# Column halves for the small products of a chunked delta-rule solve, and a first modulation sum split between TensorE and VectorE

## Chip, cores and metric

The kernel runs on one core of a Trainium2 chip. The metric is the device time of one execution in microseconds (us), a median over runs. Engines: TensorE (PE in the rows, PEld for its weight loads), VectorE (DVE), ScalarE (ACT), GpSimd (POOL), and SyncE (SP), which here only issues DMA transfers.

## What is computed

A decoder block on 512 tokens of width 1024, all in f32. Cut to the two places that matter here:

```
mod = c @ w_ada + b_ada
shift, scale, gate = split(mod, 3)
h = rmsnorm(x, pre_norm_gain) * (1.0 + scale) + shift
proj = h @ w_in                       # queries, keys, values, gates of two branches
...
# gated delta rule, 8 heads, key and value width 128, chunks of 64 tokens
lower = where(strict, (kb @ k.T) * decay, 0)
t_mat = triangular_solve(lower + eye, eye, unit_diagonal=True)
...
out = x + gate * rmsnorm(y @ w_o, post_norm_gain)
```

The queries are normalised by the root of their sum of squares per token; that sum is `ssq` below. The other branch is a sparse attention with 8 heads.

## The kernel before

**Layout.** Tokens are in four tiles of 128 (index i, NT = 4), the width in eight blocks of 128 (index k, KT = 8). PSUM is one tensor `ps` of eight banks of 512 columns. The large projections run in "units" of 128 output columns, each split into a high and a low part, so that a unit is 24 products of 512 columns (lines 723 to 725). TensorE goes through rounds; a round is a quarter of a unit (six products), and behind it come small products of the delta-rule heads, the attention and so on, at round numbers written out by hand (`solve(h, r - R_DELTA[h])`). Each engine has its own program with the same rounds; `Steps` gives every instruction of one kind a number on a semaphore, and a waiting instruction holds up all that is behind it on its engine.

**The prologue** (first 50 us). SyncE loads x, then for each block k the eight row blocks of `w_ada` for shift and scale (`mod_rows[:, k % 5, j, :]`, j = 0 to 7, in two halves of 512 KB with a semaphore each, line 511), then the first weights (line 516). The modulation of block k is a sum over 1024 rows: ScalarE scales row block 0 by its entry of c (`first_row`, line 1087) into PSUM, VectorE adds row blocks 1 to 7 (`mod_sum`, line 1607), TensorE sums over the 128 partitions by a product with ones (`modulation`, line 778), and VectorE adds the biases (`mod_columns`, lines 1613 and 1615). ScalarE then makes h of block k from x, transposed by TensorE (`turn`, line 769; h at line 1107, its high part at 1110), and the first products start (line 703). VectorE scales x's four token tiles by their norms (line 1593) before and between the sums of block 0. ScalarE's queue holds, in this order: the squares of x, `first_row(0)`, four copies of rotary tables (lines 1095, 1098), `first_split(0)`, `first_row(1)`, `first_split(1)` (line 1073), and h of block 0. VectorE's queue: sums of block 0, the first two sums of block 1, `mod_columns(0)`, the other sums of block 1.

**The solve of a head** (`solve`, one head each 33 us or so from 160 to 415 us). The inverse U of a unit triangular 128x128 block per token tile is put together from blocks of 16, 32 and 64. U and its transpose T come from DRAM with 32x32 diagonal parts done. The steps on TensorE, each over the four tiles:

- Z32 and dU32 (lines 866, 875): 32-column products on two tiles of the array on its diagonal, (rows 0 to 63, columns 0 to 31) and (rows 64 to 127, columns 64 to 95), and the like.
- `ssq` (line 889): q2 of a tile as stationary operand, a column of ones moving; result column i in bank 5. ScalarE copies it out (line 1236).
- Z64 (line 894): L times the upper right part of U, stationary 128 rows by 64 columns, result in partitions 0 to 63 of bank 3. VectorE copies it to Zs (line 1863).
- T32 (line 898): U transposed whole, 128x128, into bank 4. ScalarE copies all of it to T (line 1239).
- dU64 (line 910): T (64x64) times Zs, result in partitions 0 to 63 of bank 3; VectorE adds it to U (line 1867), which the scan of the head reads three rounds later (line 923).

vT (line 904) transposes the values in between. Which part of the array a product uses follows from where its operands and its result lie: the partitions of the operands give the rows of the array, those of the result in PSUM give the columns.

Of the kernel before, what the change touches and what calls it, by code (L numbers as in the profile page):

```python
# [15 lines left out]
P = 128  # L16
# [147 lines left out]
def program(nc, ctx, x, positions, first_cols, w_mod, w_gate, b_gate, post_gain, w_first, w_units, cst_in, cols_in, out):  # L164
# [144 lines left out]

    def o_row(t):  # L310

        return ps[:, 2 * t:2 * t + 2, :].rearrange("p a b -> p (a b)")
# [18 lines left out]
    def gvec(slot, h):  # L331
        return gsc[:, slot, :, h]

# [26 lines left out]
    def steps(name, names):  # L360
# [23 lines left out]
    pro_pe = steps("pro_pe", ["tables", "x0", "x1", "mod0"]  # L384
# [4 lines left out]
                    + ["xn0", "xn1", "xn2"] + [f"row{j}_0" for j in range(1, 4)] + ["xn3"] + [f"row{j}_0" for j in range(4, KT)]  # L389
# [305 lines left out]
    def _(pe):  # L695
# [66 lines left out]
        def turn(k):  # L762

            if k == 0:
                pe.wait_ge(*pro_dve.at(f"xn{NT - 1}"))
            if k >= 2:
                pe.wait_ge(*pro_act.at(f"h{k - 2}"))
            for i in range(NT):
                mm = pe.transpose(ps[:, 6 + k % 2, blk(i)], x_sb[:, i, blk(k)], ident)
            mm.then_inc(*pro_pe.inc(f"x{k}"))  # L770

        def modulation(k):

            if k == 0:
                pe.wait_ge(*pro_pool.at("ones"))
            pe.wait_ge(*pro_dve.at(f"row{KT - 1}_{k}"))
            for n in range(2):
                mm = pe.matmul(ps[:, 4 + k % 2, 2 * P + n:2 * P + n + 1], mod_rows[:, k % GROUPS, 0, n * P:(n + 1) * P], ones_p[:, 0:1],
                               start=True, stop=True)
            mm.then_inc(*pro_pe.inc(f"mod{k}"))  # L780

        turn(0)
        turn(1)
        modulation(0)
# [61 lines left out]
        def solve(h, rel):  # L846
# [36 lines left out]
            elif rel == 10:  # L883
# [175 lines left out]
    def _(act):  # L1059
# [23 lines left out]
        def first_row(k):  # L1083
            act.wait_ge(s_mod[k % GROUPS][0], (k // GROUPS + 1) * 16)
            if k >= 2:
                act.wait_ge(*pro_dve.at(f"scale{k - 2}"))
            act.activation(ps[:, 4 + k % 2, 0:2 * P], mod_rows[:, k % GROUPS, 0, :], ACT.Copy,
                           scale=pcol[:, 0, R_C:R_C + 1]).then_inc(*pro_act.inc(f"row{k}"))
# [136 lines left out]
        def solve(h, rel):  # L1225
# [316 lines left out]
    def _(dve):  # L1542
# [53 lines left out]
        def mod_sum(k, js):  # L1596

            acc = ps[:, 4 + k % 2, 0:2 * P]
            for j in js:
                if j == KT // 2:  # L1600
                    dve.wait_ge(s_mod[k % GROUPS][1], (k // GROUPS + 1) * 16)
                if j == 1:
# [3 lines left out]
                total = mod_rows[:, k % GROUPS, 0, :] if j == KT - 1 else acc  # L1606
# [3 lines left out]
        def mod_columns(k):  # L1610

            dve.wait_ge(*pro_pe.at(f"mod{k}"))
            dve.tensor_tensor(small_cols[:, 8 + k:9 + k], ps[:, 4 + k % 2, 2 * P:2 * P + 1], pcol[:, 0, R_BADA + k:R_BADA + k + 1],
# [228 lines left out]
        def solve(h, rel):  # L1842
# [278 lines left out]
```

## Time and profile before

| | us |
|---|---|
| median of 3 runs | 814.15 |
| lowest and highest run | 814.05, 814.99 |
| the profiled execution's own time | 814.45 |
| its span, first to last instruction | 812.5 |
| TensorE busy | 778.4 (96%) |
| VectorE busy | 444.2 (55%) |
| ScalarE busy | 338.5 (42%) |
| GpSimd busy | 400.4 (49%) |

The span leaves out what lies before the first and after the last instruction, 1.95 us here. A row of the timeline merges neighbouring instructions of one line: it gives the start of the first, the time from there to the end of the last, and their count. Since products overlap in the array, the end of one lies behind the start of the next; what a product takes from TensorE is the distance from its start to the start of the next.

### The profile page before, as it was taken

To read this page: it belongs to the slowest core of one execution; us is meant where nothing else is said; L and a number is where in the kernel's file an instruction comes from. 1 tells how busy PE (TensorE), PEld (TensorE's weight loads), DVE (VectorE), ACT (ScalarE), POOL (GpSimd) and SP (SyncE) were. 2 spreads that over 40 slices of the span, in tenths; PEclk is the share of its full clock that TensorE was granted. 3 is DMA by queue.
4 is the path that set the end of the run, shared out by engine and by line. 5 is a ranking of instruction groups with operands and counts; after the bars stand their busy time and mean duration, and the time that the engine had idled before them with its cause. 6 is when DMAs were issued, how large, how long until landed. Compare 5 with 4: busy or idle time off the path is not lost.

```text
span 812.5 us, 11490 instructions
## 1 busy us (share of the span) xinstructions
PE 778.4 (96%) x4176; PEld 631.2 (78%) x4176; DVE 444.2 (55%) x992; ACT 338.5 (42%) x719; POOL 400.4 (49%) x348
## 2 busy tenths in 40 slices
PE   2998998999999899999999999999999999999997
PEld 2877874777877688878888777778777788878997
DVE  6858779767588966877754243343334233331114
ACT  5576544534544345345344444343442432222131
POOL 3665542375545445566435254355355355434451
PEclk8899999999999999999999999999999999999999
DMA  8945545333344142312211212221222245432602
GB/s 330 413 146 190 166 96 207 102 117 103 99 87 112 66 111 92 104 66 92 78 60 71 79 53 78 78 79 55 75 85 73 95 157 187 156 129 79 230 4 103
DMA packets 69495, 95.53 MB, mean 118 GB/s; under 512 B 32936, under 2 KB 45608, under 8 KB 69440
## 3 DMA queue, kind: packets, MB, share of 16 engines
q1 hardware_dynamic: 69440, 94.81, 35.5%
q8 instruction: 33, 0.54, 0.3%
q14 instruction: 22, 0.18, 0.1%
HBM read 85.02 MB, written 9.22 MB: 116 GB/s over the span
## 4 chain that ended last, share of the span: by engine, by line
PE 78%; DVE 12%; ACT 5%; issue 2%; DMA 1%; POOL 1%; SPq 0%; DVEq 0%; POOLq 0%; ACTq 0%
PE ps L723 18%; PE ps L725 18%; PE ps L724 18%; PE ps L997 2%; PE ps L1051 2%; PE ps L1050 2%; PE ps L1049 2%; PE ps L984 2%; ACT prob L1318 2%; DVE binv L1836 2%; DVE prob L1947 1%; DVE yq L1760 1%; PE ps L991 1%; PE ps L709 1%; PE ps L703 1%
## 5 line engine op out<-in xcount | busy, mean ns | idle before, releaser
L1416 POOL TENSOR_TENSOR w_lo<-raw,w_hi 128x512 fp32r<-128x512 f32 x210 | 283.6, 1374 | 296.4 <-ACT w_hi L1069 296.4
L723 PE MATMUL ps<-h_hi,w_hi 128*128 128x512 f32 x648 | 274.3, 423 | 0.0
L725 PE MATMUL ps<-h_hi,w_lo 128*128 128x512 f32 x648 | 254.9, 393 | 0.0
L724 PE MATMUL ps<-h_lo,w_hi 128*128 128x512 f32 x648 | 254.0, 392 | 0.0
L723 PEld LDWEIGHTS ps<-h_hi,w_hi 128*128 128x128 f32 x648 | 122.5, 189 | 29.8 <-issue 9.4
L725 PEld LDWEIGHTS ps<-h_hi,w_lo 128*128 128x128 f32 x648 | 122.1, 188 | 27.5
L724 PEld LDWEIGHTS ps<-h_lo,w_hi 128*128 128x128 f32 x648 | 122.7, 189 | 21.9 <-issue 2.2
L1069 ACT ACTIVATE w_hi<-raw 128x1024 fp32r<-128x1024 f32 x105 | 109.7, 1054 | 17.1 <-PE ps L1051 17.1
L1254 ACT ACTIVATE o_tok<-ps 128x128 f32<-128x128 f32 x32 | 8.9, 278 | 89.7 <-PE ps L949 89.6
L1050 PE MATMUL ps<-w_lo,y_hi 128*128 128x256 f32 x128 | 36.2, 283 | 0.0
L1051 PE MATMUL ps<-w_hi,y_lo 128*128 128x256 f32 x128 | 36.2, 283 | 0.0
L1049 PE MATMUL ps<-w_hi,y_hi 128*128 128x256 f32 x128 | 36.2, 283 | 0.0
L1952 DVE SCALAR_TENSOR_TENSOR oat<-ps,za 128x512 f32<-128x512 f32 x8 | 5.5, 691 | 56.0 <-PE ps L997 56.0
L1346 ACT ACTIVATE y_hi<-ysum 128x512 fp32r<-128x512 f32 x8 | 5.1, 632 | 72.1 <-DVE ysum L1975 72.1
L1964 DVE SCALAR_TENSOR_TENSOR ysum<-th_b,ps 128x512 f32<-128x512 f32 x8 | 5.5, 686 | 50.4 <-PE ps L725 50.4
L1318 ACT ACTIVATE prob<-prob,amx 128x128 f32<-128x128 f32 (+3 forms) x32 | 17.6, 552 | 29.7 <-DVE amx L1940 29.7
L1753 DVE MAX8 m<-score 128x8 f32<-128x256 f32 (+2 forms) x48 | 26.4, 550 | 0.0
L1755 DVE MATCH_REPLACE8 score<-m,score 128x256 f32<-128x256 f32 (+2 forms) x48 | 26.1, 543 | 0.0
L723 PE MATMUL ps<-ob_hi,w_hi 128*128 128x512 f32 x64 | 25.1, 392 | 0.0
L723 PE MATMUL ps<-oa_hi,w_hi 128*128 128x512 f32 x64 | 25.0, 391 | 0.0
L724 PE MATMUL ps<-oa_lo,w_hi 128*128 128x512 f32 x64 | 24.9, 389 | 0.0
L724 PE MATMUL ps<-ob_lo,w_hi 128*128 128x512 f32 x64 | 24.9, 389 | 0.0
(275 smaller groups left out, 1378.5 us busy)
## 6 DMA issues: line engine op xcount, KB each, us to landing
raw<-in_w_units SPq DMA_DIRECT2D x105, 512.0 KB, 3.2
mod_rows<-in_w_mod SPq DMA_DIRECT2D x16, 512.0 KB, 8.7
inverse_tiles<-zero SPq DMA_DIRECT2D x12, 344.0 KB, 5.1
ada<-in_w_gate SPq DMA_DIRECT2D x8, 512.0 KB, 4.6
x_sb<-in_x SPq DMA_DIRECT2D x4, 512.0 KB, 6.0
first_raw<-in_w_first SPq DMA_DIRECT2D x8, 256.0 KB, 7.3
L<-gc_rows SPq DMA_DIRECT2D x8, 256.0 KB, 4.4
lower_tiles<-L SPq DMA_DIRECT2D x8, 256.0 KB, 2.7
```

Source lines behind the costliest of these rows:

```text
L723: pe.matmul(out_ap, w_hi[:, slot, k, :], rhs_hi(k), start=(k == 0), stop=False)
L724: pe.matmul(out_ap, w_hi[:, slot, k, :], rhs_lo(k), start=False, stop=False)
L725: mm = pe.matmul(out_ap, w_lo[:, slot, k, :], rhs_hi(k), start=False, stop=(k == KT - 1))
L984: pe.matmul(ps[:, SB[qt], 0:n], qk[:, 0, blk(qt)], qk[:, 1, 0:n], start=True, stop=True).then_inc(*attend_pe.inc(f"s{qt}"))
L1049: pe.matmul(o_ap, y_hi[k][:, blk(t)], w_hi[:, pair, k, :], start=(k == 0), stop=False)
L1050: pe.matmul(o_ap, y_hi[k][:, blk(t)], w_lo[:, pair, k, :], start=False, stop=False)
L1051: mm = pe.matmul(o_ap, y_lo[k][:, blk(t)], w_hi[:, pair, k, :], start=False, stop=(k == KT - 1))
L1069: act.activation(w_hi[:, slot], raw[:, slot], ACT.Copy).then_inc(hi_made, 1)
L1318: act.activation(prob[:, keys(qt)], prob[:, keys(qt)], ACT.Exp, bias=amx[:, 1, qt:qt + 1], scale=HD ** -0.5, accum_out=amx[:, 2, qt:qt + 1 ...
L1416: ins = pool.tensor_tensor(w_lo[:, slot, ks], raw[:, slot, ks], w_hi[:, slot, ks].bitcast(F32), ALU.subtract)
L1753: dve.max(m8[:, t, :], w).then_inc(*top_dve.inc(f"max{t}"))
L1755: dve.match_replace(w, m8[:, t, :], w, TAKEN).then_inc(*top_dve.inc(f"take{t}"))
```

## The change

Two edits. In the solve, `ssq` is done as two products per tile, one per half of the stationary columns, each with its result on one half of the partitions. Z64, T32 and dU64 put the results of even tiles on partitions 0 to 63 and of odd tiles on partitions 64 to 127, two tiles side by side in the columns; T32 transposes only the 64x64 corner that dU64 reads, as a product with a 64x64 identity. The copies become one of 128x128 elements (Zs, T), and the addition to U becomes two, for even and odd tiles. In the prologue, row blocks 0 to 3 of block k = 0 are summed by eight products on TensorE that take c's column as moving operand (`first_modulation`, in bank 7, ahead of the transposes); ScalarE scales row block 4 instead of 0, VectorE adds 5 to 7, and two small additions bring the direct sums into the biases (`direct_columns`). The transposes of x block 1 go behind the modulation of block 0.

```diff
-    pro_pe = steps("pro_pe", ["tables", "x0", "x1", "mod0"]
+    pro_pe = steps("pro_pe", ["tables", "direct", "x0", "mod0", "x1"]
...
-                    + ["xn0", "xn1", "xn2"] + [f"row{j}_0" for j in range(1, 4)] + ["xn3"] + [f"row{j}_0" for j in range(4, KT)]
+                    + ["xn0", "xn1", "xn2"] + [f"row{j}_0" for j in (5,)] + ["xn3"] + [f"row{j}_0" for j in (6, 7)] + ["direct0", "direct1"]
...
+    MOD_DIRECT = KT // 2
+    def first_mod(k):
+        return MOD_DIRECT if k == 0 else 0
...
+            elif k == 1:
+                pe.wait_ge(*pro_dve.at("direct1"))
...
+        def first_modulation():
+            pe.wait_ge(s_mod[0][0], 16)
+            pe.wait_ge(s_rows, 16)
+            for n in range(2):
+                for j in range(MOD_DIRECT):
+                    mm = pe.matmul(ps[:, 7, n:n + 1], mod_rows[:, 0, j, n * P:(n + 1) * P], pcol[:, 0, R_C + j:R_C + j + 1],
+                                   start=(j == 0), stop=(j == MOD_DIRECT - 1))
+            mm.then_inc(*pro_pe.inc("direct"))
+        first_modulation()
         turn(0)
+        modulation(0)
         turn(1)
-        modulation(0)
...
-                    mm = pe.matmul(ps[:, 5, i:i + 1], q2[:, blk(i)], ones[:, 0:1], start=True, stop=True)
+                    for half in (slice(0, 64), slice(64, P)):
+                        mm = pe.matmul(ps[half, 5, i:i + 1], q2_tiles[:, i, half], ones[:, 0:1], start=True, stop=True)
...
-                    mm = pe.matmul(ps[0:64, 3, upper(i)], L[:, h, i, 0:64], U[:, par, i, 64:P], start=True, stop=True)
+                    half, at = slice(64 * (i % 2), 64 * (i % 2) + 64), slice(64 * (i // 2), 64 * (i // 2) + 64)
+                    mm = pe.matmul(ps[half, 3, at], L[:, h, i, 0:64], U[:, par, i, 64:P], start=True, stop=True)
...
-                    mm = pe.transpose(ps[:, 4, blk(i)], U[:, par, i, :], ident)
+                    mm = pe.matmul(ps[half, 4, at], U[0:64, par, i, 0:64], ident[0:64, 0:64], start=True, stop=True)
...
-                    mm = pe.matmul(ps[0:64, 3, upper(i)], T[0:64, i, 0:64], Zs[0:64, i, 64:P], start=True, stop=True)
+                    mm = pe.matmul(ps[half, 3, at], T[half, i // 2, 0:64], Zs[half, i // 2, 0:64], start=True, stop=True)
...
-            act.wait_ge(s_mod[k % GROUPS][0], (k // GROUPS + 1) * 16)
+            act.wait_ge(s_mod[k % GROUPS][first_mod(k) // (KT // 2)], (k // GROUPS + 1) * 16)
...
-                act.activation(T[:], tiles(bank(4)), ACT.Copy).then_inc(*solve_act.inc("T32"))
+                act.activation(T[:, 0:2, 0:64], halves(ps[:, 4, 0:P]), ACT.Copy).then_inc(*solve_act.inc("T32"))
...
+        def direct_columns():
+            dve.wait_ge(*pro_pe.at("direct"))
+            for n, bias in ((0, pcol[:, 0, R_BADA:R_BADA + 1]), (1, small_cols[:, 16:17])):
+                at = small_cols[:, 8 + 8 * n:9 + 8 * n]
+                dve.tensor_tensor(at, ps[:, 7, n:n + 1], bias, ALU.add).then_inc(*pro_dve.inc(f"direct{n}"))
...
-        mod_sum(0, range(1, 4))
+        mod_sum(0, (5,))
         scale_rows(3)
-        mod_sum(0, range(4, KT))
+        mod_sum(0, (6, 7))
+        direct_columns()
...
-                dve.tensor_copy(Zs[0:64, :, 64:P], tiles(bank(3))[0:64, :, 64:P]).then_inc(*solve_dve.inc("Z64"))
+                dve.tensor_copy(Zs[:, 0:2, 0:64], halves(ps[:, 3, 0:P])).then_inc(*solve_dve.inc("Z64"))
...
-                dve.tensor_tensor(U[0:64, par, :, 64:P], U[0:64, par, :, 64:P], tiles(bank(3))[0:64, :, 64:P],
-                                  ALU.add).then_inc(*solve_dve.inc("U64"))
+                for odd in range(2):
+                    of_turn = U[0:64, par, odd::2, 64:P]
+                    ins = dve.tensor_tensor(of_turn, of_turn, halves(ps[64 * odd:64 * odd + 64, 3, 0:P]), ALU.add)
+                ins.then_inc(*solve_dve.inc("U64"))
```

## Rows read from the trace of the kernel before

**Rows 1.** The page: busy us, share of the span, instructions.

```profile
PE 778.4 (96%) x4176; PEld 631.2 (78%) x4176; DVE 444.2 (55%) x992; ACT 338.5 (42%) x719; POOL 400.4 (49%) x348
```

**Rows 2.** Waits of TensorE, 160-420 us: total, times, longest.

```profile
PE ps L942 <- DVE vnew L1875: 3.3, 4, 2.1
```

**Rows 3.** Timeline of TensorE, head 0: start, us, instructions; last row: cut at 173.2.

```profile
172.29 0.39 PE L724 MATMUL ps<-h_lo,w_hi 128*128 128x512 f32 x1
172.52 0.40 PE L725 MATMUL ps<-h_hi,w_lo 128*128 128x512 f32 x1
172.84 0.68 PE L894 MATMUL ps<-U,L 128*64 128x64 f32 x8
173.45 0.66 PE L898 MATMUL ps<-cst,U 128*128 128x128 f32 x4
173.86 0.48 PE L723 MATMUL ps<-h_hi,w_hi 128*128 128x512 f32 x1
...
177.26 0.68 PE L910 MATMUL ps<-Zs,T 64*64 64x64 f32 x8
177.87 0.50 PE L723 MATMUL ps<-h_hi,w_hi 128*128 128x512 f32 x1
...
172.84 0.56 PE L894 MATMUL ps<-U,L 128*64 128x64 f32 x6
```

**Rows 4.** Timeline of TensorE, head 1, around ssq.

```profile
205.40 0.95 PE L889 MATMUL ps<-cst,q 128*128 128x1 f32 x8
206.21 0.48 PE L723 MATMUL ps<-h_hi,w_hi 128*128 128x512 f32 x1
```

**Rows 5.** Timeline of TensorE: Z32 of head 0, then a Gram product.

```profile
162.81 0.44 PE L866 MATMUL ps<-U,L 64*32 64x32 f32 x16
163.18 1.16 PE L843 MATMUL ps<-kraw 128*128 128x128 f32 x8
```

**Rows 6.** The chain of waits, two places: start us, us, what.

```profile
246.80 0.40 DVE U L1867
...
279.24 0.32 DVE Zs L1863
```

**Rows 7.** Timeline, 12 to 19 us; then the load issued at 5.2.

```profile
12.47 0.48 ACT L1087 ACTIVATE ps<-mod_rows,pcol 128x256 f32<-128x256 f32 x1
...
12.98 1.54 DVE L1607 SCALAR_TENSOR_TENSOR ps<-mod_rows,pcol,ps 128x256 f32<-128x256 f32 x3
...
15.23 1.33 PE L769 MATMUL ps<-cst,x_sb 128*128 128x128 f32 x8 [2.19 <-DVE x_sb L1593]
15.71 0.45 ACT L1087 ACTIVATE ps<-mod_rows,pcol 128x256 f32<-128x256 f32 x1
...
17.06 1.01 DVE L1607 SCALAR_TENSOR_TENSOR ps<-mod_rows,pcol,ps 128x256 f32<-128x256 f32 x2
...
17.29 0.98 PE L778 MATMUL ps<-ones_p,mod_rows 128*128 128x1 f32 x4 [0.73 <-POOL first_lo L1431]
17.43 0.63 ACT L1073 ACTIVATE first_hi<-first_raw 128x512 fp32r<-128x512 f32 x1 [1.27 <-DMA first_raw<-in_w_first]
...
18.68 0.78 ACT L1107 ACTIVATE h_f<-ps,small_cols 128x512 f32<-128x512 f32 x1 [0.63 <-DVE small_cols L1615]
...
L511 SPq DMA_DIRECT2D mod_rows<-in_w_mod x1: 684/684/684, 5.2 to 5.2; - x1
...
DMA to landing us min/median/max: 8.4/8.4/8.4
```

**Rows 8.** Stretches: us, busy by engine (PE first), granted clock, DMA, GB/s.

```profile
67.50:70.50 3.00, 0.81 (x7) 0.77 (x7) 2.83 (x7) 2.97 (x8) 0.54 (x1) 1.00 0.80 261
70.50:74.00 3.50, 3.50 (x13) 2.92 (x12) 2.98 (x17) 3.47 (x11) 2.81 (x4) 0.51 0.71 275
...
263.00:266.50 3.50, 1.44 (x7) 0.82 (x5) 3.43 (x8) 0.64 (x1) 1.13 (x1) 1.00 0.38 126
16.00:26.00 10.00, 7.27 (x25) 5.87 (x24) 8.27 (x22) 5.52 (x10) 6.03 (x5) 0.50 1.03 417
```

More of the change, by code:

```diff
@@ L308, in tiles, with halves @@
         return ap.rearrange("p (i f) -> p i f", i=NT)
+    def halves(ap):
+        return ap.rearrange("p (i f) -> p i f", i=2)
+    q2_tiles = q2[:].rearrange("p (i f) -> p i f", i=NT)
     def o_row(t):
@@ L777, in modulation @@
             for n in range(2):
-                mm = pe.matmul(ps[:, 4 + k % 2, 2 * P + n:2 * P + n + 1], mod_rows[:, k % GROUPS, 0, n * P:(n + 1) * P], ones_p[:, 0:1],
-                               start=True, stop=True)
+                mm = pe.matmul(ps[:, 4 + k % 2, 2 * P + n:2 * P + n + 1], mod_rows[:, k % GROUPS, first_mod(k), n * P:(n + 1) * P],
+                               ones_p[:, 0:1], start=True, stop=True)
             mm.then_inc(*pro_pe.inc(f"mod{k}"))
+        def first_modulation():
[7 more added lines that the diff above has]
+        first_modulation()
         turn(0)
+        modulation(0)
         turn(1)
-        modulation(0)
         pe.wait_ge(*pro_act.at("cosI"))
@@ L897, in solve @@
                 for i in range(NT):
-                    mm = pe.transpose(ps[:, 4, blk(i)], U[:, par, i, :], ident)
+                    half, at = slice(64 * (i % 2), 64 * (i % 2) + 64), slice(64 * (i // 2), 64 * (i // 2) + 64)
+                    mm = pe.matmul(ps[half, 4, at], U[0:64, par, i, 0:64], ident[0:64, 0:64], start=True, stop=True)
                 mm.then_inc(*solve_pe.inc("T32"))
@@ L909, in solve @@
                 for i in range(NT):
-                    mm = pe.matmul(ps[0:64, 3, upper(i)], T[0:64, i, 0:64], Zs[0:64, i, 64:P], start=True, stop=True)
+                    half, at = slice(64 * (i % 2), 64 * (i % 2) + 64), slice(64 * (i // 2), 64 * (i // 2) + 64)
+                    mm = pe.matmul(ps[half, 3, at], T[half, i // 2, 0:64], Zs[half, i // 2, 0:64], start=True, stop=True)
                 mm.then_inc(*solve_pe.inc("dU64"))
@@ L1083, in first_row @@
         def first_row(k):
-            act.wait_ge(s_mod[k % GROUPS][0], (k // GROUPS + 1) * 16)
+            act.wait_ge(s_mod[k % GROUPS][first_mod(k) // (KT // 2)], (k // GROUPS + 1) * 16)
             if k >= 2:
                 act.wait_ge(*pro_dve.at(f"scale{k - 2}"))
-            act.activation(ps[:, 4 + k % 2, 0:2 * P], mod_rows[:, k % GROUPS, 0, :], ACT.Copy,
-                           scale=pcol[:, 0, R_C:R_C + 1]).then_inc(*pro_act.inc(f"row{k}"))
+            act.activation(ps[:, 4 + k % 2, 0:2 * P], mod_rows[:, k % GROUPS, first_mod(k), :], ACT.Copy,
+                           scale=pcol[:, 0, R_C + first_mod(k):R_C + first_mod(k) + 1]).then_inc(*pro_act.inc(f"row{k}"))
         act.wait_ge(s_rows, 16)
@@ L1599, in mod_sum @@
             for j in js:
-                if j == KT // 2:
+                if j == KT // 2 or (k == 0 and j == MOD_DIRECT + 1):
                     dve.wait_ge(s_mod[k % GROUPS][1], (k // GROUPS + 1) * 16)
-                if j == 1:
+                if j == first_mod(k) + 1:
                     dve.wait_ge(*pro_act.at(f"row{k}"))
@@ L1605, in mod_sum @@
                     dve.wait_ge(*pro_dve.at(f"row{j - 1}_{k}"))
-                total = mod_rows[:, k % GROUPS, 0, :] if j == KT - 1 else acc
+                total = mod_rows[:, k % GROUPS, first_mod(k), :] if j == KT - 1 else acc
                 dve.scalar_tensor_tensor(out=total, in0=mod_rows[:, k % GROUPS, j, :], scalar=pcol[:, 0, R_C + j:R_C + j + 1],
@@ L1610, in mod_columns @@
         def mod_columns(k):
+            if k == 0:
+                dve.wait_ge(*pro_dve.at("direct1"))
+                bias = small_cols[:, 8:9]
+            else:
+                bias = pcol[:, 0, R_BADA + k:R_BADA + k + 1]
             dve.wait_ge(*pro_pe.at(f"mod{k}"))
-            dve.tensor_tensor(small_cols[:, 8 + k:9 + k], ps[:, 4 + k % 2, 2 * P:2 * P + 1], pcol[:, 0, R_BADA + k:R_BADA + k + 1],
+            dve.tensor_tensor(small_cols[:, 8 + k:9 + k], ps[:, 4 + k % 2, 2 * P:2 * P + 1], bias,
                               ALU.add).then_inc(*pro_dve.inc(f"shift{k}"))
```

## The prediction, made before the changed kernel ran

> **What bounds the kernel now.** I read the page first. TensorE is busy for 778.4 of 812.5 us [rows 1], so the order of the work on TensorE is the time, and an edit counts by what it takes out of TensorE's queue or by the waits that it opens or closes there. The change edits two places: the solves of the eight heads (160 to 415 us) and the first 20 us. The view of waits for TensorE between 160 and 420 us gives the waits of the first place: the longest group is 3.3 us in four waits for a VectorE copy [rows 2], so TensorE is not alone in setting the pace there. The reader should keep both facts: most of what leaves TensorE's queue is time saved, but not all.
>
> **The solve of a head, instruction by instruction.** A product of two f32 operands is two records in the trace; a transpose is one. From one start to the next on TensorE, projection products follow each other every 0.23 us (172.29 to 172.52), and the first half-array block starts 0.32 us after the last one, so going from whole-array to half-array products costs 0.09 us [rows 3]. Four blocks of a head change.
>
> 1. Z64, eight records of 64 stationary columns, all on the left half: 172.84 to 173.45 is 0.61 us, changeover behind it included. Six records end at 0.56 and eight at 0.68, so one more record on the same half costs 0.06 us [rows 3]. After the change four records go to each half.
> 2. T32, four whole-array transposes: 173.45 to 173.86 is 0.41 us [rows 3]. After: four f32 products of 64x64, so eight records, four on each half.
> 3. dU64, eight records: 177.26 to 177.87 is 0.61 us [rows 3]. After: four on each half, and odd tiles also on the lower rows, so the two halves share neither rows nor columns.
> 4. ssq, eight whole-array records with one moving column: 205.40 to 206.21 is 0.81 us [rows 4]. After: sixteen records of 64 stationary columns, eight on each half, and two changeovers where there was none.
>
> The price hangs on whether the two halves work at the same time. The trace has one kind of block on different parts of the array (Z32, and dU32 alike): sixteen records of 32 columns, alternating between two tiles that share neither rows nor columns, take 162.81 to 163.18, 0.37 us [rows 5]. That is under 0.025 us a record, below half of the 0.06; so tiles that share nothing do run together. dU64 is of this kind. Z64, T32 and ssq are not: their halves share the rows. No row shows that case, so I bound it: at best both halves at once, at worst one after the other.
>
> Together: Z64 falls to 0.61 - 4 x 0.06 = 0.37 (-0.24), T32 becomes 0.37 for 0.41 (-0.04), dU64 -0.24, ssq 0.61 + 0.09 = 0.70 for 0.81 (-0.11). Sum -0.63 us; since 0.06 is rounded up and half-array blocks will now also stand before projection products that followed whole-array ones, I take -0.55. One after the other: Z64 0, T32 0.61 for 0.41 (+0.20), dU64 still -0.24, ssq 0.61 + 8 x 0.06 + 0.09 = 1.18 for 0.81 (+0.37); with the same rounding +0.35. I take the first end as the likelier: [rows 5] is the nearest block, and all it lacks is a shared row.
>
> One more row speaks on shared rows. Eight whole-array records with 128 moving columns take 1.16 us to the end of the last [rows 5], against 0.95 with one moving column [rows 4]. If a weight load had to wait until the product in flight on the same rows was through, eight times 128 columns would have added far more than 0.21. The Trainium skill (TensorE: Matmul & The Clock Gate, Part 3: Packing small matmuls) says against this change that a weight load overlaps with products in flight only where the row groups differ; by that rule ssq, Z64 and T32 would run one half after the other, which is the first rival below. The same notes (TensorEngine Tiling (Array Packing), Key Properties) say that different tiles load and multiply in parallel and that a change of mode drains the array; by that the first end holds, and the trace's 0.09 us is the drain.
>
> **Times eight heads, less what is off the path.** -0.55 x 8 = -4.4 us. The chain of waits leaves TensorE twice where edited blocks stand: at 246.80 it is on VectorE's add for head 2, behind a copy that waited for the block ahead of dU64, so head 2's dU64 is beside it; at 279.24 it is on VectorE, as in the five us before it, so ssq, Z64 and T32 of head 3 are beside it too [rows 6]. That is one head's worth: -3.9 left. Elsewhere the stalls of [rows 2] may swallow some more, since VectorE's own queue hardly gets shorter. I take 0.4 off for it: -3.5.
>
> **VectorE and ScalarE.** The Zs copy shrinks from 64x256 to 128x128 elements, about 0.1 us less and on the chain only once [rows 6]; the add to U becomes two adds of 64x128, about 0.1 us more, as the second overlaps with the first. T's copy on ScalarE falls to a quarter; the work beside it hides this either way, the next reader of T comes two rounds later. Together 0, ends -0.5 and +0.8 (eight times 0.1, were all adds on the path).
>
> **The first 20 us.** Before: ScalarE scales row block 0 at 12.47, VectorE adds seven more from 12.98 on, TensorE sums over partitions at 17.29 for 0.98, and 0.41 us later ScalarE makes h at 18.68 [rows 7]. The change takes four of the eight row blocks from VectorE: about 2 us of sums (0.5 each, [rows 7]) go, and TensorE does sixteen records of the direct sum in its pause of 2.19 us before x's transposes at 15.23 [rows 7], where they fit (sixteen at 0.1 are under 2). It looks like 2 us gained. It isn't, since ScalarE now starts with row block 4, which is in the second half of the load: issued at 5.2, landed 8.4 later, 13.6 [rows 7]. So ScalarE's first row moves from 12.47 to about 13.65, and its queue behind it (four table copies, the first weight split, row 0 of group 1) by about 1.05, as that queue had only gaps of 0.1: row 0 of group 1 starts at 16.75 instead of 15.71 and ends at 17.2. VectorE now: its first sum starts at 14.2 instead of 12.98, and four sums are gone, so it is through with group 0 some 0.8 us sooner, at 16.3 to 16.4. But then it stands before the first two sums of group 1, which wait for ScalarE's 17.2, and the shift and scale of group 0 are queued behind those: 17.2 + 1.01 = 18.2, + 0.41 = 18.6 to 18.7 against 18.68. ScalarE's second weight split lands at 17.43 whatever happens and ends at 18.06, another floor [rows 7]. So the prologue gives 0, with ends -0.6 (that floor) and +0.5 (a slower ScalarE queue). The transposes of x block 1 move behind the modulation of block 0 and wait for the direct column adds; their one reader is h of block 1, which ScalarE makes after h of block 0, its high part and a weight split, so they cost nothing. SyncE's queue keeps its order, and the loads that wait for a modulation wait for one that is no later.
>
> **Sum.** 814.45 us is the profiled execution's own time (span 812.5 and 1.95 around it); the median of the three runs is 814.15, 0.3 less. -3.5 + 0 + 0 makes 810.95 for an execution like the profiled one, and 810.6 against the median. That is my figure.
>
> **Rivals.**
> The halves work one after the other (slower). Place: ssq and T32 of each head. +0.35 x 8 = 2.8, less the head's worth beside the path, 2.5: 816.6 us. It decides from the point where a record on one half holds the other up by more than about 0.6 of its 0.06 us; there gain and loss meet. For it: no row has halves on shared rows. Against it: [rows 5], and weight loads that hide behind products on the same rows.
>
> VectorE sets the pace of heads 0 to 3. Its waits there [rows 2] grow by what TensorE saves; only heads 4 to 7 pay, 4 x 0.55 = 2.2: 811.9 us, and 812.7 with the adds of U on the path. For it: the chain is on VectorE at both places of [rows 6]. Against: both lie in heads 2 and 3, and all eight heads' VectorE work waits in turn for TensorE's blocks.
>
> TensorE's granted clock. It is 0.50 from 16 to 26 us, and again 0.51 from 70.5 to 74, after three microseconds with only 0.81 busy; it did not fall after the stretch at 263 with 1.44 of 3.5 busy [rows 8]. If TensorE arrives at that stall 1.5 us sooner and waits longer, the clock (2.4 GHz) may fall to 1.2 there too: half of 3.4 us, +1.7, so 812.3. Conversely the direct products fill the pause at 13 us; were the low stretch before 26 us to end 3.4 us sooner, -1.7: 808.9.
>
> The edit of the first stage backfires alone (ScalarE's queue longer than reckoned) by 0.5: 811.1.
>
> **Chances.** Forecast with its small terms 0.50; clock falling or VectorE's pace 0.22, of which two thirds still end over 0.2% faster; halves in turn 0.22; the clock sooner 0.06. A measurement of this kernel can't tell less than about 0.2%, 1.6 us, from no change. So faster 0.67, same 0.12, slower 0.21. The range has to reach into the slower case to leave out no more than 0.2: 809.2 to 816.8; the forecast's own range is 809.2 to 812.0.
>
> **What would show it.** ssq from first start to the next projection product about 0.70 us (1.2 if in turn), Z64 and dU64 0.37, T32 0.37 (0.61 if in turn); starts of records on the two halves a few ns apart. VectorE's first sum near 14.2, h at 18.6 to 18.7, the first projection product no more than 0.3 us sooner or later than before. The stalls at 200, 264 and 280 longer by what TensorE saved before them. Wrong would be: T32 or ssq longer than now; a new low-clock stretch; a first product 0.6 us sooner or more.

## The result, and the profile after

The changed kernel takes 809.69 us, the median of six runs (808.73 to 811.99), beside 814.1 for the kernel before on the same chip (six runs, 813.93 to 815.53). The ratio is 0.9944, 95% interval 0.993 to 0.9958: 3.4 to 5.7 us less, 4.4 by the medians. The profiled execution took 810.23 us, 4.2 less than the one before. Forecast were 3.5 us less, 810.6, in a range of 809.2 to 816.8.

The page, span and busy time, answers to [rows 1]:

```profile
span 808.3 us, 11722 instructions
PE 776.9 (96%) x4288; PEld 628.5 (78%) x4288; DVE 445.3 (55%) x998; ACT 336.3 (42%) x719; POOL 398.1 (49%) x348
```

TensorE does 112 records more in 1.5 us less. Its busy time fell by less than the span, since the direct sum adds 3.4 us of work to what was a pause at 13 us; the page alone would not tell where 4.2 us went. The timeline does. L920 is Z64, L925 T32 and L938 dU64 of head 0, L914 ssq of head 1; this answers to [rows 3, 4]:

```profile
171.84 0.45 PE L920 MATMUL ps<-U,L 128*64 128x64 f32 x8
172.22 0.45 PE L925 MATMUL ps<-cst,U 64*64 64x64 f32 x8
172.60 0.50 PE L735 MATMUL ps<-h_hi,w_hi 128*128 128x512 f32 x1
...
176.25 0.45 PE L938 MATMUL ps<-Zs,T 64*64 64x64 f32 x8
176.63 0.50 PE L735 MATMUL ps<-h_hi,w_hi 128*128 128x512 f32 x1
...
203.89 0.39 PE L977 MATMUL ps<-vnew,intra 128*128 128x128 f32 x2
204.21 0.63 PE L914 MATMUL ps<-cst,q 128*64 128x1 f32 x16
204.77 0.50 PE L735 MATMUL ps<-h_hi,w_hi 128*128 128x512 f32 x1
```

From start to start: ssq 0.56 (204.21 to 204.77) where it was 0.81, Z64 0.38 for 0.61, T32 0.38 for 0.41, dU64 0.38 for 0.61. Against ssq stand 0.09 ahead of it: its first record starts 0.32 behind the first record of the product before it (203.89 to 204.21), where ssq followed in 0.23 before (205.17 to 205.40). The eight heads agree to 0.01. One head is shorter by 0.16 + 0.23 + 0.03 + 0.23 = 0.65 us, eight by 5.2. The halves work at the same time, on shared rows as well. In the profiled executions the time between one projection product and another, the same two in both kernels, was 297.75 us before (155.91 to 453.66) and is 293.77 now (155.63 to 449.40): 4.0 of the 4.2 us lie in the stretch of the solves.

TensorE's waits between 155 and 420 us, total, times, longest, answer to [rows 2], and behind them the second of them in the timeline, in head 3:

```profile
PE ps L970 <- DVE vnew L1917: 4.0, 4, 2.0
PE ps L931 <- DVE yv L1805: 1.1, 1, 1.1
```

```profile
279.01 0.66 PE L931 MATMUL ps<-cst,yv 128*128 128x128 f32 x4 [1.15 <-DVE yv L1805]
```

VectorE's queue has not got shorter, TensorE comes to it sooner and waits longer: 0.7 us more in the first group, all of it at one place in head 2 (0.31 at 253.35 before, 1.04 at 251.61 now), and 0.6 more in the second, which was 0.5 in the same view of before. The waits at 200 (1.13) and 264 us (2.08 before, 2.04 now) did not grow. Per head VectorE's queue is even 0.14 longer: the two adds to U hold it for 0.60 us before its next instruction starts (244.57 to 245.17) where the one add took 0.33 (246.80 to 247.13), and the copy to Zs takes 0.29 instead of 0.42. How much of the longer waits is due to that, the trace does not tell. A wait of ssq of head 0 for VectorE, 0.5 before, is gone, so the waits grew by about 0.9 together.

The first 20 us, answering to [rows 7]:

```profile
13.26 3.41 PE L801 MATMUL ps<-pcol,mod_rows 128*128 128x1 f32 x16
13.78 0.48 ACT L1115 ACTIVATE ps<-mod_rows,pcol 128x256 f32<-128x256 f32 x1 [1.26 <-DMA mod_rows<-in_w_mod]
...
16.81 0.46 ACT L1115 ACTIVATE ps<-mod_rows,pcol 128x256 f32<-128x256 f32 x1
17.30 1.01 DVE L1635 SCALAR_TENSOR_TENSOR ps<-mod_rows,pcol,ps 128x256 f32<-128x256 f32 x2 [0.37 <-ACT ps L1115]
...
18.75 0.78 ACT L1135 ACTIVATE h_f<-ps,small_cols 128x512 f32<-128x512 f32 x1 [0.61 <-DVE small_cols L1648]
```

TensorE gives the direct sum 3.41 us and turns x at 16.53 instead of 15.23; still h starts at 18.75, against 18.68. ScalarE's wait for the second half of the load (1.26 us, to 13.78) and the two sums of group 1 at 17.30, behind which shift and scale are queued, take back what four sums less would give.

### The profile page after: what moved, and what is told of

It is laid out like the page before. It is cut to its first block, busy times and chain, and to the rows that moved or that the text cites. A ratio compares the mean times of both kernels' runs of the same rounds, so it can differ in the third digit from the quotient of the medians.

```text
span 808.3 us, 11722 instructions
## 1 busy us (share of the span) xinstructions
PE 776.9 (96%) x4288; PEld 628.5 (78%) x4288; DVE 445.3 (55%) x998; ACT 336.3 (42%) x719; POOL 398.1 (49%) x348
## 4 chain that ended last, share of the span: by engine, by line
PE 79%; DVE 10%; ACT 4%; DMA 3%; issue 2%; POOL 1%; SPq 1%; DVEq 0%; POOLq 0%; ACTq 0%
PE ps L735 19%; PE ps L737 18%; PE ps L736 18%; PE ps L1025 2%; PE ps L1079 2%; PE ps L1078 2%; PE ps L1077 2%; PE ps L1012 2%; ACT prob L1346 2%; DVE prob L1989 1%; DVE binv L1876 1%; DMA mod_rows<-in_w_mod 1%; PE ps L1019 1%; PE ps L867 1%; PE ps L852 1%
```

## The experiments

They ask, in this order: what each edit is worth alone; whether the halves run together or the block is shorter for another reason; whether waits for VectorE swallow what TensorE saves; and what a better version would be. Each run is beside runs of the kernel before on its chip, with medians of 814.6 to 814.8.

### The first-stage edit alone

All solve code is that of the kernel before.

```diff
-                    for half in (slice(0, 64), slice(64, P)):
-                        mm = pe.matmul(ps[half, 5, i:i + 1], q2_tiles[:, i, half], ones[:, 0:1], start=True, stop=True)
+                    mm = pe.matmul(ps[:, 5, i:i + 1], q2[:, blk(i)], ones[:, 0:1], start=True, stop=True)
...
```

> Only the prologue edit (direct sum of four row blocks on TensorE), the solve as before. My theory: the first row of ScalarE waits for the second half of the load and the first two sums of block 1 stand before the shift and scale of block 0, so h of block 0 starts at 18.6 to 18.8 us, as before; time 814.1 us, within 0.5. Rival: the prologue gave the extra microsecond by which the change beat my figure: about 813.2 us, h of block 0 at 17.8.

Measured: 813.68 us (twelve runs, 811.09 to 815.04), 1.1 less than the median of before (814.75), ratio 0.9988 with 0.9977 to 0.9999: between 0.1 and 1.9 us less. Its timeline:

```profile
12.89 1.84 PE L801 MATMUL ps<-pcol,mod_rows 128*128 128x1 f32 x16
13.50 0.48 ACT L1111 ACTIVATE ps<-mod_rows,pcol 128x256 f32<-128x256 f32 x1 [1.37 <-DMA mod_rows<-in_w_mod]
...
17.01 1.01 DVE L1631 SCALAR_TENSOR_TENSOR ps<-mod_rows,pcol,ps 128x256 f32<-128x256 f32 x2 [0.72 <-ACT ps L1111]
...
18.30 0.78 ACT L1131 ACTIVATE h_f<-ps,small_cols 128x512 f32<-128x512 f32 x1 [0.45 <-PE ps L783]
```

Neither expectation is met as it stands: h starts at 18.30, 0.3 us ahead of the theory's range and 0.5 behind the rival's 17.8, and the median lies nearer to the rival's gain than to none. The chain has the same links as in the changed kernel, each 0.3 to 0.45 us sooner (13.50 for 13.78, 17.01 for 17.30, 18.30 for 18.75), and the first of them is the landing of the load. Over the six profiled kernels with this first stage h starts between 18.30 and 18.79, over the two with the old one at 18.62 and 18.68. And what h gains does not last: the first of the ordinary projection products (L723 before) starts at 52.03 here and at 52.13 before, and one at 156 us is 0.2 later here (156.08 for 155.91). The 0.5 us by which this profiled execution is the shorter come later; most of it is the wait of ssq of head 0 for VectorE, 0.48 before, which is there in the profiles with the old first stage and in none with the new one. Of the median's 1.1 us a part is the clock: five of the twelve runs here have a mean granted clock of 0.995, against one of the seventeen before; at 0.992 the medians are 814.61 and 814.95. So this edit is worth a few tenths, and the 2 us that four sums seem to promise are not there.

The direct sum costs 0.115 us a record here and 0.21 in the changed kernel, where TensorE's transposes ahead of it follow each other in 0.21 us at 13 us, and here in 0.11. That is the clock at its higher and its lower level. The changed kernel's profile has no record of the clock before 25.3 us, so that this is read from the pace: the first products follow in 0.42 to 0.43 us before 25 us and in 0.23 behind it. It decided nothing, since h waits for other things.

### The solve edit alone

The modulation of group 0 is that of the kernel before.

```diff
-    MOD_DIRECT = KT // 2
...
-        first_modulation()
         turn(0)
-        modulation(0)
         turn(1)
+        modulation(0)
```

> Only the solve edit, the prologue as before. My theory: all of the gain, 809.7 us (809 to 810.5). Rival: a third of the gain or more is the prologue's: 810.8 us or more.

Measured: 810.38 us (six runs, 809.33 to 811.73), ratio 0.9953 with 0.9939 to 0.9966, that is 2.8 to 5.0 less, 3.8 in the middle (4.4 by the medians), inside the 809 to 810.5 expected. The solve brings nearly all of the gain. A stretch of this kernel, in the columns of [rows 8]:

```profile
264.30:267.80 3.50, 3.50 (x26) 2.92 (x27) 2.46 (x7) 1.80 (x3) 0.03 (x1) 0.51 0.07 27
```

In this execution the granted clock fell to the lower level for 3.5 us behind the stall at 262, where the kernel before and the changed one kept the higher. That is the rival about the clock, seen in one execution. It cost less than the 1.7 us of the rival's reckoning: between two projection products around that stretch this kernel takes 44.69 us (247.25 to 291.94) and the changed one 44.60 (247.02 to 291.62), since the wait at 251 us is 0.27 here and 1.04 there. In the kernel with the varied ssq below the clock fell at the same place, and there the same two products are 45.86 us apart (244.72 to 290.58), 1.3 more.

### The price of a record on one half

Heads 4 to 6 get an ssq with other records; those that repeat write the same results again. In head 7 the last edit goes over Z64, T32 and dU64: both even tiles first (four records on the left half), then both odd ones.

```diff
-                for i in range(NT):
-                    for half in (slice(0, 64), slice(64, P)):
+                products = [(i, half) for i in range(NT) for half in (left, right)]
+                if h == 4:
+                    products = products + products
+                elif h == 5:
+                    products = products + [(i, left) for i in range(NT)] * 2
+                elif h == 6:
+                    products = [(i, half) for half in (left, right) for i in range(NT)]
...
-                for i in range(NT):
+                for i in range(NT) if h != 7 else (0, 2, 1, 3):
```

> The changed kernel with the ssq block varied by head, results unchanged: head 4 does its eight products twice (32 records, alternating halves), head 5 does the eight and then eight more on the left half alone (32 records), head 6 does all left halves first and then all right ones, head 7 orders Z64, T32 and dU64 as even tiles first, odd tiles after. Halves on shared rows in parallel: head 4's block 0.56 + 0.46 = 1.02 us from first start to the next product; head 5's 0.56 + 16 x 0.058 = 1.49 us; head 6's 0.56 if weight loads reach far enough ahead, 1.0 if the order of the program decides; head 7's Z64, T32, dU64 0.38 each or up to 0.60 by the same alternative. If the halves took turns and the shorter block came from something else, heads 4 and 5 would cost the same.

Measured, ssq of heads 4, 5 and 6 and then Z64 and T32 of head 7 (one execution, 810.85 us):

```profile
305.16 1.10 PE L921 MATMUL ps<-cst,q 128*64 128x1 f32 x32
306.19 0.50 PE L735 MATMUL ps<-h_hi,w_hi 128*128 128x512 f32 x1
...
337.66 1.56 PE L921 MATMUL ps<-cst,q 128*64 128x1 f32 x32
339.15 0.50 PE L735 MATMUL ps<-h_hi,w_hi 128*128 128x512 f32 x1
...
371.70 0.89 PE L921 MATMUL ps<-cst,q 128*64 128x1 f32 x16
372.52 0.50 PE L735 MATMUL ps<-h_hi,w_hi 128*128 128x512 f32 x1
...
405.89 0.46 PE L927 MATMUL ps<-U,L 128*64 128x64 f32 x8
406.28 0.46 PE L932 MATMUL ps<-cst,U 64*64 64x64 f32 x8
406.66 0.50 PE L735 MATMUL ps<-h_hi,w_hi 128*128 128x512 f32 x1
```

Sixteen records more on alternating halves take 1.03 - 0.56 = 0.47, 0.029 each; sixteen more on the left half alone take 1.49 - 0.56 = 0.93, 0.058 each. The same number of records, half the time: the halves run side by side, and ssq's rows are shared; records on the two halves start 7 ns apart. This settles the first rival. By the rule of the Trainium skill (TensorE: Matmul & The Clock Gate, Part 3: Packing small matmuls) that a weight load overlaps with products in flight only where the row groups differ, both heads would have taken 1.49, and the trace disagrees. The Trainium skill's other page (TensorEngine Tiling (Array Packing), Key Properties) has different tiles load and multiply in parallel, and the trace agrees with that.

Head 6 has the records of the changed kernel, first the eight of the left half and then the eight of the right, and takes 0.82 instead of 0.56. The starts of its records show why: four on the left 0.058 apart, then the last four on the left side by side with the first four on the right, then four on the right alone. Head 7 has four on the left and then four on the right, and Z64, T32 and dU64 still take 0.39, 0.38 and 0.39, as with alternating tiles; there the starts on the two halves are 13 ns apart. So it is not only neighbours that overlap. The order of the program matters once a group is longer than these four records: with eight and eight most of what the halves give was lost, with four and four nothing.

### A longer ssq in heads 3 and 5

```diff
-                for i in range(NT):
+                for i in range(NT) if h not in (3, 5) else (0, 1, 2, 3) * 3:
```

> The changed kernel with the ssq products of heads 3 and 5 done three times over (48 records for 16), results unchanged, so about 0.92 us more for TensorE in each. Theory that head 3's block lies beside the path: the stall of 1.15 us before the transposes of v in head 3 (L931 at 279.0) shrinks to about 0.2 and head 3's dU64 still starts within 0.2 of 281.43, while head 5's dU64 and all that follows come 0.9 later: about +1.0 us in all. Rival, TensorE is the path in both: +1.85 us.

Measured (one execution, 809.81 us). Head 3 of this kernel:

```profile
272.17 1.57 PE L914 MATMUL ps<-cst,q 128*64 128x1 f32 x48
273.67 0.50 PE L735 MATMUL ps<-h_hi,w_hi 128*128 128x512 f32 x1
...
277.62 0.66 PE L931 MATMUL ps<-cst,yv 128*128 128x128 f32 x4
...
280.04 0.45 PE L938 MATMUL ps<-Zs,T 64*64 64x64 f32 x8
```

head 5 of it:

```profile
336.84 1.57 PE L914 MATMUL ps<-cst,q 128*64 128x1 f32 x48
...
344.54 0.45 PE L938 MATMUL ps<-Zs,T 64*64 64x64 f32 x8
```

and both heads of the changed kernel:

```profile
273.31 0.63 PE L914 MATMUL ps<-cst,q 128*64 128x1 f32 x16
...
281.43 0.39 PE L938 MATMUL ps<-Zs,T 64*64 64x64 f32 x6
...
338.22 0.63 PE L914 MATMUL ps<-cst,q 128*64 128x1 f32 x16
...
344.99 0.45 PE L938 MATMUL ps<-Zs,T 64*64 64x64 f32 x8
```

The block is 0.94 us longer in both heads (1.50 for 0.56). From ssq to dU64, head 5 takes 7.70 for 6.77, all 0.93 of it paid; head 3 takes 7.87 for 8.12, and the stall of 1.15 ahead of the value transposes is gone. In head 3, then, 0.94 us on TensorE cost nothing, and what is saved there only makes the wait longer; in head 5 it counts in full. This is the step "beside the path" of the prediction, shown by adding instead of taking away. The expected 1.0 us in all can't be read from the whole time of one execution, 809.81, since the clock's level in the first 25 us moves it by as much.

### ssq next to Z64

ssq moves one round later, right ahead of Z64, so that one change of the array's layout serves both.

```diff
-            elif rel == 10:
+            elif rel == 11:
...
-            elif rel == 11:
```

> The changed kernel with ssq moved one round later, directly ahead of Z64 (TensorE and ScalarE alike), so that two blocks of half-array products stand together. Theory that going between whole-array and half-array products costs about 0.09 us each way: two of them go, ssq and Z64 together take 0.19 us a head less, 8 x 0.19 = 1.5 less 0.2 beside the path: 808.4 us. Rival, the gap belongs to the block and not to the change of form: no difference, 809.7; or ScalarE's later copy of ssq delays the transposes of v (a wait at L931): slower.

Measured: 809.09 us (six runs, 808.25 to 810.04), ratio 0.9936 with 0.9923 to 0.9949; 0.6 less than the changed kernel, where 1.3 were expected, and within what two medians differ by. Head 1:

```profile
205.50 0.63 PE L914 MATMUL ps<-cst,q 128*64 128x1 f32 x16
205.98 0.43 PE L919 MATMUL ps<-U,L 128*64 128x64 f32 x8
206.34 0.45 PE L924 MATMUL ps<-cst,U 64*64 64x64 f32 x8
206.72 0.50 PE L735 MATMUL ps<-h_hi,w_hi 128*128 128x512 f32 x1
```

and its waits:

```profile
PE ps L969 <- DVE vnew L1915: 4.2, 4, 2.1
PE ps L930 <- DVE yv L1803: 1.7, 2, 1.2
```

ssq, Z64 and T32 take 1.22 us where they took 0.56 + 0.38 + 0.38 = 1.32, and one entrance of 0.09 is saved: 0.19 a head, 1.5 in eight. The two waits grew by 0.8 against the changed kernel. What the changeover is worth on TensorE is shown; what it is worth in time is not clear. The medians say 0.6 us, as if half of it went into waits for VectorE, while in the profiled executions the stretch of the solves is 1.8 shorter than in the changed kernel (156 to 449 us), and the profiled execution, 808.25, is the fastest of the six.

### The direct sum with two row blocks

ScalarE then starts with row block 2, in the first half of the load.

```diff
-    MOD_DIRECT = KT // 2
+    MOD_DIRECT = KT // 4
...
-        mod_sum(0, (5,))
+        mod_sum(0, (3,))
...
-        mod_sum(0, (6, 7))
+        mod_sum(0, (4, 5, 6, 7))
```

> The changed kernel with two row blocks of the first modulation group summed by TensorE instead of four, so ScalarE starts with row block 2, which is in the first half of the load, and VectorE adds 3 to 7. Theory that the prologue's gain was lost to ScalarE's wait for the second half: ScalarE's first row at 12.4 again, h of block 0 at 18.1 (floor: ScalarE's second weight split), 0.5 to 0.6 us sooner than 18.75, time about 809.1 us. Rival, VectorE's two more sums take it back: h at 18.6 or later, 809.7 us.

Measured: 809.94 us (six runs, 809.46 to 811.83), ratio 0.995 with 0.9936 to 0.9964, no gain over the changed kernel.

```profile
12.93 0.48 ACT L1115 ACTIVATE ps<-mod_rows,pcol 128x256 f32<-128x256 f32 x1 [0.15 <-DMA mod_rows<-in_w_mod]
...
17.42 1.00 DVE L1635 SCALAR_TENSOR_TENSOR ps<-mod_rows,pcol,ps 128x256 f32<-128x256 f32 x2
...
18.83 0.78 ACT L1135 ACTIVATE h_f<-ps,small_cols 128x512 f32<-128x512 f32 x1 [0.28 <-DVE small_cols L1648]
```

ScalarE's first row does come 0.85 us sooner than in the changed kernel (12.93 for 13.78), but two sums more keep VectorE with group 0 until 17.4, where its first two sums of group 1 follow (17.42), and h starts at 18.83. So the wait for the load is not the only thing that holds h: take it away, and VectorE's own queue is next, in this execution at almost the same time. That queue was late here for a reason outside the edit: VectorE scales x's last token tile only at 14.65, after a wait of 0.32 for its norm from GpSimd. In the two kernels below that have the same first stage it did so at 13.65 and 13.38, and h started at 17.90 and 17.81. There the theory's 18.1 is met and passed, and its rival is met in this one; the six runs together show no gain.

### Products that nobody reads, in three stalls

TensorE waits about 2 us at 68, 132 and 264 us, and behind the first two the granted clock is low. Products of parts of h into unused banks are put ahead of those waits; their results are not used.

```diff
+        def fill(out_ap, count):
+            n = out_ap.shape[-1]
+            for _ in range(count):
+                pe.matmul(out_ap, h_hi[:, 0, 0:P], h_hi[:, 0, 0:n], start=True, stop=True)
...
+                if m == 6:
+                    pe.wait_ge(*gram_dve.at("L", 0))
+                    fill(bank(5), 6)
...
+            if h == 0:
+                pe.wait_ge(*small_act.at("gcT"))
+                fill(bank(7), 6)
...
+                if (h, i) == (2, 2):
+                    fill(ps[:, 7, 2 * P:4 * P], 12)
```

> The changed kernel with products that nothing reads in three stalls of TensorE of about 2 us (before the first Gram product, before the seventh index logit, in the scan of head 2), 1.4 us of them each, so that they end inside the stall. Theory that the low clock behind such a stall follows from TensorE's rest in it: no low stretch at 70 and 135 us, 2 x 1.7 = 3.4 us gained, 806.3 us, and no run with a third low stretch near 264 us. Rival, the clock falls for another reason or the products delay what waits behind them: 809.7 us or more.

Measured: 807.22 us (six runs, 806.22 to 807.71), ratio 0.9911 with 0.9897 to 0.9925, 2.5 less than the changed kernel, where 3.4 were expected. Stretches of the changed kernel, then of this one (columns as in [rows 8]):

```profile
69.70:73.10 3.40, 3.40 (x13) 3.01 (x13) 2.53 (x14) 3.37 (x9) 2.31 (x3) 0.51 0.64 241
134.50:137.90 3.40, 3.40 (x12) 2.00 (x10) 3.16 (x7) 1.60 (x3) 1.32 (x2) 0.50 0.00 0
```

```profile
69.70:73.20 3.50, 3.50 (x23) 3.06 (x22) 3.36 (x22) 3.47 (x11) 2.85 (x4) 1.00 0.68 264
133.65:137.05 3.40, 3.40 (x10) 1.48 (x9) 3.23 (x7) 1.29 (x3) 2.56 (x2) 0.50 0.02 5
```

The first low stretch is gone, the second is not. Its products missed the stall:

```profile
119.93 1.52 PE L841 MATMUL ps<-h_hi 128*128 128x512 f32 x6
...
132.10 0.70 PE L861 MATMUL ps<-kpad,iq 64*128 64x256 f32 x4 [1.97 <-DVE score L1785]
```

They ran at 119.93; the stall, 1.97 us, comes some groups of logits later, before the thirteenth. The third fill cut the wait at 264 us from 2.04 to 0.62, and the clock stayed high there, as it also did in the changed kernel without a fill. One caution: the kernel with the varied ssq above kept the high level behind its whole stall of 2.39 us at 68, so one profile without a low stretch does not prove the fill's effect; the three filled kernels together are the evidence.

### All three together

```diff
-            elif rel == 10:
+            elif rel == 11:
...
-    MOD_DIRECT = KT // 2
+    MOD_DIRECT = KT // 4
...
+                    fill(bank(5), 6)
...
```

> The three edits together: if they add up, 809.7 - 1.3 - 0.6 - 3.4 = 804.4 us; if moving ssq or the filling opens a new wait, 806 or more.

Measured: 804.88 us (five runs, 803.99 to 805.68), ratio 0.9886 with 0.9872 to 0.99. This beats both kernels: 4.8 less than the changed one. The three edits alone came to -0.6, +0.25 and -2.5, 2.8 in all; so by the medians 2.0 of the 4.8 us are more than the sum. The profiled executions show where they differ, by the starts of the same projection products: 1.3 us less than the changed kernel by 50 us (50.42 for 51.75), 2.9 by 89 us, 2.7 by 156 us and 4.6 by 449 us. The 804.88 come near the 804.4 expected, but not for the reason given, since none of the three parts alone gave what was put into that sum. The first 1.3 us are the likely source of most of the surplus: the first product starts at 19.46, 0.9 sooner than in the changed kernel (20.34), where the direct sum of two by itself had it at 20.41 (the late norms described there), and the clock reaches its higher level at 23.5 and not at 25.3 us. The rest is the stall at 68 us, 1.5 (1.7 in the kernel with the fills alone), and 1.9 in the solves. Why the early clock differs from one execution to the next stays open.

### The third fill moved into its stall

```diff
-                if m == 6:
+                if m == 12:
```

> The kernel of the run before with one edit: the six unused products that stood before the seventh logit (TensorE ran them at 119.93, in no stall) now stand before the thirteenth, in front of which TensorE waits 1.97 us for VectorE. Theory (the granted clock falls a few us after a stall of about 2 us, for 3.4 us, and half of those are lost): the products cover 1.4 to 1.5 us of the stall, 0.5 to 0.6 of it is left, the low stretch at 133 to 136 is gone (granted 1.00 there), and they no longer cost 1.5 us where they stood. So 1.7 back from the clock, and up to 1.4 back from the place where they filled nothing: 804.9 - 1.7 = 803.2 if the stall there grows by what the old place gives back, 801.8 if it does not; I expect 803.2. Rival (the low stretch comes from what the cores of the chip do in all, or at set times, not from this stall): it stays, and the time is 804.9 to 803.5 without a change of the clock at 133 to 136.

Measured: 804.77 us (six runs, 804.47 to 805.17), ratio 0.9887 with 0.9866 to 0.9908. The stall and the stretch behind it, in this kernel:

```profile
130.07 1.53 PE L841 MATMUL ps<-h_hi 128*128 128x512 f32 x6
132.22 0.70 PE L861 MATMUL ps<-kpad,iq 64*128 64x256 f32 x4 [0.62 <-DVE score L1783]
```

```profile
132.70:136.10 3.40, 3.40 (x17) 2.03 (x15) 3.16 (x7) 2.32 (x5) 1.50 (x2) 1.00 0.00 0
```

Stall 0.62 and clock 1.00, as the theory says; the median, though, is that of the kernel before it within 0.1 us, where 1.7 less were expected. At the place itself the 1.7 us are there. Between two projection products, the same in both kernels, the profiled execution of the kernel before it takes 27.17 us (115.03 to 142.20) and this one 25.46 (116.03 to 141.49). But by its first ordinary projection product this execution is already 1.1 us later (51.54 for 50.42), since its clock stays at the lower level until 25.9 us instead of 23.5; so the whole is 0.7 less, 804.85 for 805.59.

For the medians there is only the mean granted clock of each run. The kernel with the misplaced fill had 0.992 in two of its five runs, at 805.59 (the profiled one, with the low stretch at 133 us) and 805.68, and 0.998 to 1.0 in the other three, at 803.99 to 804.88. If the low stretch at 133 us was missing in those three, its median is that of a run without one, and a fill there had nothing to give back. The mean does not tell where the clock was low, so this is likely and not shown.

That the misplaced products had cost little where they stood is shown: between 115 and 128 us (115.03 to 127.70, and 116.03 to 128.56) they cost 0.14 us. Without them TensorE waits 0.44 and 0.63 us for VectorE at 124 and 127 us, and with them it waited nowhere there.

## Why the prediction was right

**What bounds the kernel.** Right: what left TensorE's queue was saved, except where VectorE was late. The longer ssq showed both sides, 0.93 of 0.93 paid in head 5 and none in head 3.

**The solve of a head.** The four terms were forecast at -0.24, -0.04, -0.24 and -0.11, -0.63 together, and measured at -0.23, -0.03, -0.23 and -0.16, -0.65. The near bound was the right one, and the end taken was right: what [rows 5] lacked, a shared row, made no difference. (The far bound adds up to +0.33, given as +0.35 "with the same rounding"; the rounding of the near one, 0.08, would have made it +0.41.) Too low was the step behind the sum, 0.55 "taken" for 0.63 on account of rounding and of half-array blocks ahead of projection products. The second reason exists but is small: the product behind such a block is followed after 0.33 us (172.60 to 172.93) and was before, behind a whole-array block, after 0.32. ssq itself was put at 0.61, the time of Z64 before, and takes 0.56.

**Times eight, less what is off the path.** Taken were 4.4 - 0.5 - 0.4 = 3.5. Measured are 5.2 (0.65 a head), less 0.9 by which the waits grew, 4.3; the profiled executions have 4.0 between the same products, and the 0.3 between the two are not placed. The solve alone gave 3.8, with 2.8 to 5.0 as its interval. So the allowance of 0.9 was right in size, and in heads 2 and 3, where the chain had put it: a stall at 252 (head 2) and one at 279 (head 3). The list of signs was less exact: it named the stalls at 200, 264 and 280, and of these only the last grew.

**VectorE and ScalarE** were put at nothing. One price in it was too low: the second add holds VectorE for 0.27 us a head, not 0.1, while the copy to Zs saves 0.13 as foreseen. On the whole time no run tried them apart from the rest, so that their sum was nothing is not shown.

**The first 20 us.** Right in its links and in the end: ScalarE's first row forecast at 13.65 and found at 13.78, its row of group 1 at 16.75 and 16.81, h at 18.6 to 18.7 and 18.75. Wrong in one step that had no effect: sixteen direct records were to fit into the pause before x's transposes at "under 2" us, and took 3.41, as the clock was at its lower level; the transposes moved by 1.3 us. The first projection product started at 20.34, before at 20.27. The term 0 was within its ends for h, but the edit alone measured 0.1 to 1.9 less, so it may be worth some tenths in most runs. The chain starts with a load's landing, 13.50 in one execution and 13.78 in another. What the prediction did not look for is a gain outside the first 20 us, at the wait of head 0's ssq, 0.5 us.

**The rivals.** Halves in turn: out, by 0.029 against 0.058 us a record. VectorE sets the pace of heads 0 to 3: partly so, 0.9 of 5.2 us, not half of it. A clock that falls behind the stall at 264: not in the profiled execution of the changed kernel, but in that of the solve edit alone and in that of the kernel with the varied ssq. It is a matter of the single run, and the prediction was too sure in making it one of the kernel; its price, 1.7 us, was too high, as part of the loss only shortens waits (0.1 us in the one execution, 1.3 in the other). The slowest runs of the solve alone (811.73) and of the changed kernel (811.99) lie where this rival puts the time, but no profile shows where their clock was low. The first stage backfiring: no.

So the forecast was short by 0.7 (profiled executions) to 0.9 us (medians), and the term that was mis-sized is the saving of a head: 0.65, not 0.55, 0.8 in eight heads. That the two agree to a tenth is in part luck, since some tenths of the first stage and the 0.3 above are of the same size. The range was wide on the upper side for one rival that no row of before could exclude; that was its honest width.

## What to carry to other kernels

Small f32 products with at most 64 stationary columns are worth splitting over the two column halves, with instructions on different halves close to each other: groups of four records a half cost nothing here, groups of eight lost most of it. Count what TensorE saves head by head, and then look for the next stall in each: a microsecond saved ahead of a wait for VectorE is worth nothing, and adding work there is a cheap way to test that. Read such small edits from the starts of the same products in two traces: the level of the clock in the first 25 us moved the whole time here by as much as the edits did. Of a reduction moved to another engine, follow the whole queue of every engine up to the next common consumer before putting a price on it.

## What the runs showed of the hardware

- A record of 64 f32 stationary columns with one moving column takes 0.058 us on one half and 0.029 on alternating halves with the same rows; with the halves grouped eight and eight, sixteen take 0.82 us instead of 0.56; grouped four and four, eight take 0.38 to 0.39 as they do with alternating tiles.
- Going from whole-array to half-array products costs 0.09 us, and between two kinds of half-array blocks nearly nothing (ssq 0.48 ahead of Z64, 0.56 ahead of a projection product).
- Stalls of TensorE of about 2 us were followed by 3.4 us or so at a granted clock of 0.5, but not always. Over the profiled kernels that had the stall whole (2.0 to 2.5 us), this happened at 68 us in seven of eight, at 132 us in ten of ten, at 264 us in two of eight. Where products that nobody reads had cut it to 0.6 to 1.0 us, it happened in none of seven. The low stretch cost 1.7 us at 132 us; at 264 us it cost 0.1 in one execution and 1.3 in another, as waits for VectorE took up part of it.
- A record of 128 stationary columns with one moving column took 0.115 us in one execution and 0.21 in another, at the same place of the program: in the first 25 us the clock's level differs from one execution to the next.
